# Half of the attention's value product moved ahead of its norm in a two-block transformer kernel

## What is computed

```python
h = rmsnorm(x, norm_g)            # x * rsqrt(mean(x*x) + EPS) * norm_g
proj = h @ w_in                   # 10256 columns
aq, ak, av, az, bqk, bv, bi, bf, bo, bz, ga, gb = jnp.split(proj, idx, axis=-1)
q = rope(rmsnorm(two_map_heads(aq), q_norm_g), cos, sin)
k = rope(rmsnorm(two_map_heads(ak), k_norm_g), cos, sin)
v = av.reshape(bsz, s, A_HEADS, A_V_DIM).transpose(0, 2, 1, 3)
```

## Time and profile before

| what | value |
|---|---|
| runs | 1796.04, 1796.82, 1798.45 us |
| the profiled execution, own time | 1797.98 us |
| its span in the profile | 1796.1 us |
| granted TensorE clock, mean | 0.984 |
| TensorE busy | 1731.1 us |
| VectorE (DVE), ScalarE (ACT), GpSimd (POOL) busy | 1127.6, 924.6, 459.8 us |
| DMA | 255.28 MB, 142 GB/s |

### The profile page before, as it was taken

The page is one execution under the profiler, slowest core; times in us unless marked ns, Lnnn a source line. Parts: engine busy times, 40 slices in busy tenths (PEclk is TensorE's granted clock), DMA queues, the critical chain, the costliest instruction groups (busy, mean ns, idle before and its releaser), DMA issues.

```text
span 1796.1 us, 29026 instructions
## 1 busy us (share of the span) xinstructions
PE 1731.1 (96%) x10836; PEld 1433.7 (80%) x10836; DVE 1127.6 (63%) x2007; ACT 924.6 (51%) x1968; POOL 459.8 (26%) x864
## 2 busy tenths in 40 slices
PE   6999998999999999988999989999999899999998
PEld 3453566888888876557999988899899898998998
DVE  4228866888878333685555577686556675785555
ACT  3237653525252523674555565575554564664542
POOL 1016001000000020320000134067771161287730
PEclk9999999999999998998999999999999999999999
DMA  9323332455555321202554443524345335433351
GB/s 341 139 94 122 135 120 94 141 187 188 188 188 188 141 74 47 95 1 94 188 187 175 171 147 124 196 99 142 136 142 187 142 107 199 144 127 141 120 193 42
DMA packets 127541, 255.28 MB, mean 142 GB/s; under 512 B 2462, under 2 KB 7212, under 8 KB 127404
## 3 DMA queue, kind: packets, MB, share of 16 engines
q1 hardware_dynamic: 126406, 251.16, 39.3%
q0 software_dynamic: 704, 2.10, 0.4%
q10 hardware_dynamic: 294, 0.18, 0.0%
HBM read 252.38 MB, written 1.05 MB: 141 GB/s over the span
## 4 chain that ended last, share of the span: by engine, by line
PE 51%; DVE 1%; ACT 1%; issue 0%; POOL 0%; DVEq 0%; ACTq 0%
PE ps L1189 12%; PE ps L1191 12%; PE ps L1190 12%; PE ps L1436 2%; PE ps L1434 2%; PE ps L1435 2%; PE ps L1514 1%; PE ps L1517 1%; PE ps L1509 1%; PE ps L1090 1%; PE ps L1063 1%; PE ps L1480 1%; PE ps L1204 0%; PE ps L1205 0%; ACT big_r L1623 0%; DVE big_r L2091 0%
## 5 line engine op out<-in xcount | busy, mean ns | idle before, releaser
L2091 DVE TENSOR_TENSOR big_r<-ring,big_r 128x1024 fp32r<-128x1024 f32 x214 | 263.9, 1233 | 249.3 <-ACT big_r L1623 249.2
L1623 ACT ACTIVATE big_r<-ring 128x1024 fp32r<-128x1024 f32 x214 | 226.2, 1058 | 370.8 <-PE ps L1191 358.3
L1190 PE MATMUL ps<-big_r 128*128 128x256 f32 (+1 forms) x1088 | 360.6, 331 | 0.0
L1189 PE MATMUL ps<-hT_r,big_r 128*128 128x256 f32 (+1 forms) x848 | 270.6, 319 | 0.0
L1191 PE MATMUL ps<-hT_r,big_r 128*128 128x256 f32 (+1 forms) x848 | 265.6, 313 | 0.0
L1189 PE MATMUL ps<-big_r 128*128 128x256 f32 (+1 forms) x720 | 239.9, 333 | 1.4 <-DVE big_r L2277 1.4
L1191 PE MATMUL ps<-big_r 128*128 128x256 f32 (+1 forms) x720 | 237.9, 330 | 0.0
L930 POOL TENSOR_TENSOR sq<-sq 128x256 f32<-128x256 f32 (+1 forms) x30 | 36.1, 1202 | 730.4 <-ACT sq L1583 730.2
L1190 PEld LDWEIGHTS ps<-big_r 128*128 128x128 f32 x1088 | 206.8, 190 | 18.7
L1191 PEld LDWEIGHTS ps<-hT_r,big_r 128*128 128x128 f32 x848 | 161.5, 190 | 9.6
L1189 PEld LDWEIGHTS ps<-hT_r,big_r 128*128 128x128 f32 x848 | 161.6, 191 | 9.3 <-issue 0.2
(11 more groups left out here) (319 smaller groups left out, 4280.7 us busy)
## 6 DMA issues: line engine op xcount, KB each, us to landing
ring<-in_w_in SPq DMA_DIRECT2D x44, 2048.0 KB, 7.7
ring<-in_w_mlp SPq DMA_DIRECT2D x32, 2048.0 KB, 7.9
ring<-in_w_mod SPq DMA_DIRECT2D x24, 2048.0 KB, 8.0
ring<-in_w_out SPq DMA_DIRECT2D x4, 2048.0 KB, 9.0
ring<-in_w_out_a SPq DMA_DIRECT2D x4, 2048.0 KB, 7.8
ring<-in_w_out_b SPq DMA_DIRECT2D x4, 2048.0 KB, 7.8
ring<-in_w_o SPq DMA_DIRECT2D x4, 2048.0 KB, 7.8
ring<-in_w_in SPq DMA_DIRECT2D x2, 1152.0 KB, 11.0
```

What stands on the lines that cost most here:

```text
L1189: mm(b[:, 0:T], w_hi[:, k, :], hi(k), start=(j == 0), stop=False)
L1190: mm(b[:, 0:T], w_hi[:, k, :], lo(k), start=False, stop=False)
L1623: act_fn(hi, raw, ACT.Copy).then_inc(hi_ready, 1)
L2091: V.tensor_tensor(lo, raw, hi.bitcast(F32), ALU.subtract).then_inc(lo_ready, 1)
```

## The change

At each entry, TensorE starts with the first half of av (512 columns, four granules) on activations that have the norm's gain but not its root: ACT writes `xT` times gain as high part g_hi (`gained`), DVE the rest g_lo (`gained_rest`), chunk by chunk while the stage before still runs. The sums of squares and lambda stand between the first and the second of these granules. Two transposes then bring the token roots, which lie along the free axis, onto the partitions (the bank `roots`); ACT copies them to `small` and applies them as a scale per partition when it copies the two av banks out. The order of granules becomes av first half (numbers 0 to 3), aq (4 to 11), ak (12 to 19), av second half (20 to 23), bif, bv. The splits of granules 3, 4 and 5 now stand inside the loop over the eight normed chunks: on ACT ahead of chunks 0, 3 and 6, on DVE at k = 2, 5 and 8. In the tail between the rotations the second half of av takes the place of the first. The lines of DVE's `run_units`, that quoted above included, are unchanged. Cut to its core:

```diff
+        for n in range(2):
+            take((tag, "av", n), (2 if l == 0 else 6) + n)
         take((tag, "lam"), 5)
         take((tag, "n1"), 4)
+        take((tag, "roots"), 5)
         unit_plan(tag, units_b())
-        for n in range(4):
-            take((tag, "av", n), n)
+        for n in range(2, 4):
+            take((tag, "av", n), n - 2)
...
-BEFORE = ("aq", "ak", "av", "bif", "bv")
+BEFORE = (("av", 0), ("aq", 0), ("aq", 1), ("ak", 0), ("ak", 1), ("av", 1), ("bif", 0), ("bv", 0), ("bv", 1))
...
-                return ("b", ("h" if j < n_before else "norms", "end" if j < n_after else "mqk", "spare")[j % B_BUFS])
+                last = "end" if j < n_after else "mqk"
+                others = ("spare", last) if l == 0 else (last, "spare")
+                return ("b", (("h" if j < n_before else "norms",) + others)[j % B_BUFS])
...
+                for m in range(4):
+                    pe.wait_ge(g_ready, KC * l + 2 * m + 2)
+                    tokens_granule("av", 0, m, g_hi[l], g_lo[l])
+                    if m == 0:
+                        summed_squares((tag, "n1"), SEQ)
+                        key = (tag, "lam")
+                        b = start_bank(key)
+                        pe.wait_ge(lam_prod, l + 1)
+                        fill(mm(b[:, 0:2], cc("ones", HD), small[0:HD, 16:18], start=True, stop=True), key)
+                key = (tag, "roots")
+                b = start_bank(key)
+                pe.wait_ge(nt_ready, nt_before[l] + 1)
+                for t in range(2):
+                    last = tr(b[:, t * P:(t + 1) * P], rstd[:, root_slot[l], t * P:(t + 1) * P], IDENT)
+                fill(last, key)
...
-                run_units(tag, units_b(), main, [lambda m=m: tokens_granule("av", 0, m) for m in range(B_BUFS)])
-                tokens_product("av", B_BUFS)
+                run_units(tag, units_b(), main, [lambda m=m: tokens_granule("av", 1, m, hb1_hi, hb1_lo) for m in range(B_BUFS)])
+                tokens_product("av", 4 + B_BUFS)
...
+            def gained(l, k):
+
+                act_fn(g_hi[l][:, k, :], xT[:, k, LAT:TOK], ACT.Copy, scale=gain(DEPTH + l, RB["g"] + k))\
+                    .then_inc(g_hi_ready, 1)
...
-                        if i == DEPTH - 1 and key[3] == KC - 2:
-                            hi_to(first_gran["b", 0] + 1)
+                        if i == DEPTH - 1:
+                            gained(0, key[3] - 1)
+                        if i == DEPTH - 1 and KC - 3 <= key[3] < KC - 1:
+                            hi_to(first_gran["b", 0] + key[3] - KC + 4)
...
                 square_summed((tag, "n1"), KC - 1, last + (KC - 1,), LAT)
-                hi_to(first_gran["b", l] + 2)
+                gained(l, KC - 1)
+                hi_to(first_gran["b", l] + 3)
                 reciprocal_root((tag, "n1"), P, SEQ, D)
-                hi_to(first_gran["b", l] + 3)
                 await_bank(act, (tag, "lam"))
                 drain(act_fn(small[:, 0:2], bank((tag, "lam"))[:, 0:2], ACT.Exp), (tag, "lam"))
                 for k in range(KC):
                     nts[0] += 1
                     act.wait_ge(nt_ready, nts[0])
+                    if k in (0, 3, 6):
+                        hi_to(first_gran["b", l] + 4 + k // 3)
                     act_fn(hb1_hi[:, k, :], nt[:, k % 2, 0:SEQ], ACT.Copy).then_inc(h_hi_ready, 1)
+                await_bank(act, (tag, "roots"))
+                roots = bank((tag, "roots"))[:, 0:SEQ].rearrange("p (t q) -> p t q", t=2)[:, :, 0]
+                drain(act_fn(small[:, 20:22], roots, ACT.Copy), (tag, "roots"))
+                await_drained(act, (tag, "roots"))
+                for n in range(2):
+                    key = (tag, "av", n)
+                    await_bank(act, key)
+                    drain(act_fn(av_tok[:, n, 0:512], bank(key)[:, :], ACT.Copy, scale=small[:, 20 + n:21 + n]), key)
                 run_units(tag, units_b())
...
+                def tokens_copy(name, dst, first=0):
+                    for n in range(first, 4):
...
-                tokens_copy("av", av_tok)
+                tokens_copy("av", av_tok, 2)
...
+            def gained_rest(n):
+                while n_gained[0] < n:
+                    l, k = divmod(n_gained[0], KC)
+                    n_gained[0] += 1
+                    dve.wait_ge(g_hi_ready, n_gained[0])
+                    V.scalar_tensor_tensor(g_lo[l][:, k, :], xT[:, k, LAT:TOK], gain(DEPTH + l, RB["g"] + k),
+                                           g_hi[l][:, k, :].bitcast(F32), ALU.mult, ALU.subtract).then_inc(g_ready, 1)
...
-                        if i == DEPTH - 1 and key[2] == BLOCKS - 1 and key[3] == KC - 2:
-                            lo_to(first_gran["b", 0] + 1)
+                        if i == DEPTH - 1 and key[2] == BLOCKS - 1 and key[3] >= 2:
+                            gained_rest(key[3] - 1)
+                        if i == DEPTH - 1 and key[2] == BLOCKS - 1 and KC - 3 <= key[3] < KC - 1:
+                            lo_to(first_gran["b", 0] + key[3] - KC + 4)
...
-                lo_to(first_gran["b", l] + 2)
+                gained_rest(KC * (l + 1))
+                lo_to(first_gran["b", l] + 3)
                 n = newton((tag, "n1"), P, SEQ, D)
                 for k in range(KC + 2):
+                    if k in (2, 5, 8):
+                        lo_to(first_gran["b", l] + 4 + k // 3)
                     if k >= 2:
                         h_his[0] += 1
                         dve.wait_ge(h_hi_ready, h_his[0])
...
-                lo_to(first_gran["b", l] + 3)
...
+                    if l < DEPTH - 1 and c >= 2:
+                        gained_rest(KC * (l + 1) + c - 1)
```

More of the change, by code:

```diff
@@ L361, in granules_b @@
     before = []
-    for name in BEFORE:
+    for name, n in BEFORE:
         if name == "bif":
@@ L366, in granules_b @@
             continue
[L367 to L373, removed]
+        for m in range(4):
+            if name in ("av", "bv"):
+                product = (b, name, 2 * n + 1) if m == 3 else None
+            else:
+                product = (b, f"{name}{4 * n + m}", 0)
+            before.append(((name, l, n), m, product))
     mid = [((name, l, c // 4), c % 4, (b, name, c)) for name, c in MID]
@@ L395, in plan_slots @@
     for l in range(DEPTH):
-        for name in BEFORE:
-            slots += [(name, l, n) for n in range(1 if name == "bif" else 2)]
+        slots += [(name, l, n) for name, n in BEFORE]
         slots += [(name, l, n) for name, n in MID_SLOTS]
@@ L536, in program @@
         u_hi, u_lo = over(5), xT_r[:, :, 0:SEQ]
+        g_hi, g_lo = (over(4), over(3)), (over(5), over(6))
         def pair(region):
@@ L1406, in _, with tokens_granule @@
                 tag = ("b", l)
-                summed_squares((tag, "n1"), SEQ)
-                key = (tag, "lam")
+                def tokens_granule(name, n, m, x_hi, x_lo):
+                    keys = [(tag, name, 2 * n + t) for t in range(2)]
+                    banks = [start_bank(key) if m == 0 else bank(key) for key in keys]
+                    g = gran_no[(name, l, n), m]
+                    pe.wait_ge(lo_ready, g + 1)
+                    w_hi, w_lo = gran_bufs[g]
+                    for t in range(2):
+                        o = banks[t].rearrange("p (a c) -> p a c", a=4)
+                        for k in range(2):
+                            x0, x1 = (x[:, 2 * m + k, t * P:(t + 1) * P] for x in (x_hi, x_lo))
+                            y_hi, y_lo = (w[:, 4 * k:4 * k + 4, :] for w in (w_hi, w_lo))
+                            mm(o, x0, y_hi, start=(m == 0 and k == 0), stop=False)
+                            mm(o, x0, y_lo, start=False, stop=False)
+                            last = mm(o, x1, y_hi, start=False, stop=(m == 3 and k == 1))
+                        if m == 3:
+                            fill(last, keys[t])
+                    if m < 3:
+                        last.then_inc(gran_used, 1)
+                for m in range(4):
+                    pe.wait_ge(g_ready, KC * l + 2 * m + 2)
[7 more added lines that the diff above has]
+                key = (tag, "roots")
                 b = start_bank(key)
-                pe.wait_ge(lam_prod, l + 1)
-                fill(mm(b[:, 0:2], cc("ones", HD), small[0:HD, 16:18], start=True, stop=True), key)
+                pe.wait_ge(nt_ready, nt_before[l] + 1)
+                for t in range(2):
+                    last = tr(b[:, t * P:(t + 1) * P], rstd[:, root_slot[l], t * P:(t + 1) * P], IDENT)
+                fill(last, key)
                 source[0] = (h_ready, h_seen[0], 1)
@@ L1420, in main @@
                         split_product(gran_of[(tag, name, 0)], h_hi_at, h_lo_at, SEQ)
[L1422 to L1439, removed]
-                        last.then_inc(gran_used, 1)
                 def tokens_product(name, first=0):
                     for g in range(first, 8):
-                        tokens_granule(name, g // 4, g % 4)
```

(10 more changed lines are left out.)

10 lines of the change are left out of this document (7 added, 3 removed).

## The result

The changed kernel takes **1807.54 us** in the median of four runs (1806.82 to 1810.82), the kernel before beside it 1797.63 (four runs, three of them those given at the start). The ratio is 1.0059, with a 95% interval of 1.0047 to 1.0072: slower, as forecast, and 1.9 us above the forecast of 1805.6. The profiled execution took 1806.94 by its own time, with a span of 1805.1 against 1796.1.

A forecast was written before the change was run, and what follows sets the result against it. TensorE was taken to bound the kernel, busy 1731.1 of 1796.1 us. Entry +2.1 and tail +2.3 us made 4.4 a layer, 8.8 for both, giving 1805.6 us, range 1800 to 1811.5.

The forecast's parts named there:

- T: At each entry, the end of the last product of the stage before; the forecast counts its times from there.
- The work ahead of T: In the stage before, the gained chunks' extra ACT and DVE work lies under TensorE's products: costed at nothing.
- The covered wait: At the entry, TensorE goes on at T with av's first half, without the 1.40 us wait, free at T + 12.6.
- What is late next: Ahead of aq0, three splits in DVE's loop take 10.9 us in sum; TensorE stands 4.6 us, until T + 17.2.
- The cold restart: Behind the 4.6 us wait, aq0 and aq1 restart at the slow clock: 1.8 us, between 0 and 2.15.
- A second gap: Ahead of aq2, granule 6 is split only behind ACT's wait for aq0's bank: 2.35 us late, range 2.2 to 2.5.
- A third gap: In the tail, granule 23 is split only after both sines, making av's last granule late: +2.3 us, 2.1 to 2.4.
- longer end: In the tail, the split takes 1.52 us beside POOL's rotary work, where alone it takes 1.23.
- The sum: Over entry and tail, 4.4 us for a layer, 8.8 for both, everything else being the same work.
- the bounds: For a layer, 2.1 us with no cold restart and short ends, 5.4 with long ends and a chain 0.5 longer.
- 13.6 us to be had: At the entries before the change, some 5 us of waits and about 1.8 of slow clock each, 13.6 in all.
- every gap cooling TensorE: Rival: gaps ahead of aq2 and in the tail also cost 1.8 more each; 8.0 a layer, 1812.8 us, chance 0.06.

The follow-up runs named there:

- e2_g6: Changed kernel with granule 6 (for aq2) split right behind the loop over the chunks, ahead of the wait for aq0's bank: 1801.6 us, ratio 1.0020.
- e1_tail: Changed kernel with DVE's look-ahead line in the tail again naming the granule behind the tail (second half of av): 1804.99 us, ratio 1.0036.
- e6_all: Changed kernel with the edits of e1_tail, e2_g6 and e4_g3_early, and aq0 run by itself ahead of aq1: 1786.20 us, ratio 0.9932.
- e5_both: Changed kernel with the edits of e1_tail and e2_g6 together: 1798.12 us, ratio 0.9994 to the kernel before.
- e4_g3_early: Changed kernel with granule 3 split ahead of the norm's root, not inside the loop over the chunks: 1804.11 us, ratio 1.0032.

## Why the prediction was right

The causes came as forecast, the sizes nearly so. In the order of its steps, T counted as there:

- **The work ahead of T, at nothing**: right. The gained chunks alone gave 0.9998.
- **The covered wait**: right. The transposes end at T + 12.62 (forecast 12.6). On the way there the forecast's T + 9.3 for granules 1 and 2 is a slip: with 2.76 for granule 3 it gives 12.1 and not its 12.3; the trace has 9.5 and 12.2. The squares' 1.40 us wait is gone.
- **What is late next**: right in time and in cause. DVE's chain took 10.97 us (10.9), with waits for ACT of 0.73, 0.27 and 0.27 (0.75, 0.35, 0.35); aq0 starts at T + 17.19 and 17.20 (17.2), a wait of 4.57 and 4.56 (4.6).
- **The cold restart, 1.8** (what the slow clock behind the wait costs): the term that was mis-sized. It measured 2.69 and 2.54. The step that failed is "between the 1.48 and 2.15 measured": these were read off a stretch in which TensorE was also held by DVE's chunks and by granule 2's split, so they were no price of the clock. Here six of the eight chunks are ready when aq0 starts and the last two 0.4 us later, nothing else holds TensorE, and each matmul at the slow clock counts in full: 5.9 us behind the restart with one every 0.213 us in place of 0.120 lose 2.6, by estimate. How long the slow stretch lasts also varies, and how much of it lies in the wait: 3.5 us where it cost 1.28 (e2_g6, 7.04 us for what takes 5.76), 7 us where it cost 2.7, and 7 us of which 2.5 lay ahead of the restart where it cost 1.9 (e1_tail, second entry).
- **A second gap, 2.35**: right. The idle time is 2.21 and 2.22; counted as in the forecast, from where the next matmul would have started (0.12 behind the last one, at 1057.21), aq2 is 2.37 late at the first entry. Its place and releaser are as forecast. With both terms the entry came to +2.97 in the mean (16.95 against 13.98), not +2.1.
- **A third gap, +2.3**: 2.0. The split began 0.38 us behind the rotations' end (0.40), took 1.22 and reached TensorE 0.05 later (0.15):

```profile
1122.43 1.22 DVE L2128 TENSOR_TENSOR big_r<-ring,big_r 128x1024 fp32r<-128x1024 f32 x1
```

The longer end of its length, 1.52, was not met, though POOL's rotary work stood beside this split too:

```profile
1122.51 1.73 POOL L950 TENSOR_TENSOR big<-big,rs 128x256 f32<-128x256 f32 x1
```

It began 0.08 us behind the split and took 1.73 us itself, where the same line took 0.74 at 1119.30. In e1_tail a POOL instruction was running since 1119.51 when the split began at 1119.81, and there the split took 1.52. The Trainium skill (GPSIMD Engine Reference, Specifications) has POOL and DVE contend when the DVE instruction has two SBUF inputs. The trace agrees at both places, but the forecast's step from there to the longer end doesn't follow: here POOL was the one held up.

- **The sum**: 8.8 forecast. The trace gives 2.97 + 2.0 for a layer, 9.9, less the 0.9 by which the first block happened to be shorter; the medians differ by 9.9. By its own terms the bounds add to 2.25 and 5.5 a layer, where it has 2.1 and 5.4. That the sum came so near is luck in part: the clock was 0.8 a layer too small and the third gap 0.3 too large. The other 0.8 of the 1.9 us is the kernel before, at 1797.63 in the median here and at 1796.82 in the forecast.
- **"13.6 us to be had"**, in the first part, was too much. The waits are there, but removing the slow clock of the kernel before brought 0.00 and 1.06 us at aq2 and no time that can be measured (0.9998). e6_all, which removes most of the waits, gets 11.2 by the spans.
- **The rivals**: every gap cooling TensorE did not happen in the profiled execution of the kernel after, but the wait of 2.2 us did it in six of the ten times that it stands in these kernels ahead of aq2, at 1.5 us each (aq2 to bif 68.4 us in place of 66.9). The forecast's argument against it, that TensorE was busy for longer ahead of this gap, is not borne out. What decides between the two is left open.

The Trainium skill (TensorE: Matmul & The Clock Gate, Why this matters for your kernels) asks to leave no long idle gaps between bursts of matmuls. For the 4.6 us wait the trace agrees at each of its eight places without filler, where it cost between 1.3 and 2.7 us. That a wait of 2.2 us was enough in six of ten is read from these runs alone.

## What to carry to other kernels

When work is moved ahead of a wait, count what the consumer behind it then asks for in full: here the covered product asked for two granules' splits, and it was these, put into the producer's loop, that ended the wait, not the norm. Work that is renumbered takes its look-ahead lines with it; an index that says "the old first half + 3" makes no error when the order changes, only a late granule. That line and the granule that nothing split ahead of aq0's bank together cost 8.6 us by the spans (e5_both), where the whole idea gained 11.2 (e6_all). Take the price of a slow clock from a stretch where nothing but TensorE sets the pace, or fill the wait with idle transposes and see what comes back.

## What the runs showed of the hardware

- Behind the same wait of 4.6 us, with the same work, the granted clock stood at 0.50 for 3.5 us in some places and for some 7 in others (e2_g6 twice 3.5, after twice 7, e5_both 6.5 and 3.5). This makes up to 1.4 us an entry, and with it differences of a few us between versions that a sum of waits doesn't give. Each is read from one execution. The kernel before alone lay between 1795.69 and 1800.85 us in 23 runs, its four slowest with a mean granted clock of 0.983, its four fastest with 0.985 to 0.987, so a few us between two single traces need not come from the edit.
- By the length of TensorE's wait at the entries and in the tails: 4.6 us brought the clock down at eight of eight places, 3.59 at four of four, 2.9 at one of two (e4_g3_early), 2.2 ahead of aq2 at six of ten, 1.73 at one of two, 1.65 at none of ten. Each stretch behind a 2.2 us wait lasted 3 to 3.5 us at 0.50 and cost 1.5.
- Transposes of a constant hold the clock up: 38 took 4.31 us, 0.113 each. They brought 2.6 us an entry where all inputs were ready, and 28 brought nothing at the first entry of the kernel before, where DVE set the pace.
- POOL and DVE side by side: an addition of POOL took 1.73 us in place of 0.74 beside a weight split of 1.22, and 1.60 beside one of 1.52.
